# One kernel, a two-layer block and a hybrid layer: the chunk products of an HGRN2 recurrence cut into blocks of 32 keys

## The reference, cut to what matters

```python
def chunk_step(state, inp):
    qc, kc, vc, gc = inp
    b = jnp.cumsum(gc, axis=2)
    o_inter = jnp.einsum('bhck,bhkv->bhcv', qc * jnp.exp(b), state)
    diff = b[:, :, :, None, :] - b[:, :, None, :, :]
    decay = jnp.exp(jnp.where(causal, diff, -jnp.inf))
    scores = jnp.einsum('bhtk,bhsk,bhtsk->bhts', qc, kc, decay)
    o_intra = jnp.einsum('bhts,bhsv->bhtv', scores, vc)
    ...
```

## Time and profile before

| | |
|---|---|
| median of 3 runs | 2142.12 us (2141.5 to 2142.12) |
| the profiled execution | 2141.52 us, span from first to last instruction 2139.7 us |
| TensorE busy | 2123.4 us, 99% of the span |
| DVE, ACT, GpSimd (POOL) busy | 997.5, 744.0, 1133.7 us |
| mean granted TensorE clock | 0.999 |
| the recurrence | 77.7 to about 257 us |

### The profile page before, as it was taken

How to read it: one execution, slowest core, us unless ns; L and a number is a source line. 1 busy time by engine, 2 the same in 40 slices (tenths; PEclk the granted TensorE clock), 3 DMA queues, 4 the chain that set the end, 5 groups by cost and what they waited for, 6 DMA issues and landing times.

```text
span 2139.7 us, 26103 instructions
## 1 busy us (share of the span) xinstructions
PE 2123.4 (99%) x10184; PEld 1769.7 (83%) x10184; DVE 997.5 (47%) x1137; ACT 744.0 (35%) x850; POOL 1133.7 (53%) x814
## 2 busy tenths in 40 slices
PE   9999999999999999999999999999999999999998
PEld 7888888888888888978888888888888888888887
DVE  6255554555313165444545422744477545553226
ACT  5234442222223355544222232524543332222244
POOL 6565545555545433355555555544566555555553
PEclk9999999999999999999999999999999999999999
DMA  5221122222233212223222232222222222223321
GB/s 177 78 79 60 40 89 98 92 96 97 99 118 108 99 60 79 79 100 117 98 98 98 92 105 98 99 98 98 98 98 98 82 99 96 97 98 108 117 99 59
DMA packets 31567, 203.20 MB, mean 95 GB/s; under 512 B 3336, under 2 KB 5640, under 8 KB 7696
## 3 DMA queue, kind: packets, MB, share of 16 engines
q1 hardware_dynamic: 31504, 202.30, 27.3%
HBM read 200.19 MB, written 2.10 MB: 95 GB/s over the span
## 4 chain that ended last, share of the span: by engine, by line
PE 94%; DVE 2%; ACT 2%; POOL 1%; DMA 1%; issue 0%; SPq 0%; DVEq 0%; ACTq 0%; POOLq 0%
PE bank L1741 93%; POOL w_lo L604 1%; DMA raw<-wall 1%; ACT w_hi L680 0%; DVE x L1624 0%; PE bank L2078 0%; DVE sgate L1673 0%; DVE aqk L1452 0%; DVE bank L1449 0%; DVE rot L1450 0%; DVE ssq L1190 0%; DVE h L1674 0%; DVE ssq L1698 0%; PE bank L2099 0%; ACT rstd L680 0%
## 5 line engine op out<-in xcount | busy, mean ns | idle before, releaser
L585 POOL TENSOR_TENSOR w_lo<-raw,w_hi 128x512 fp32r<-128x512 f32 x680 | 979.9, 1472 | 875.9 <-ACT w_hi L680 875.9
L1741 PE MATMUL bank<-u_hi,w_hi 128*128 128x512 f32 (+1 forms) x1968 | 770.7, 392 | 2.2 <-DVE u_lo L1177 1.2
L1741 PE MATMUL bank<-u_lo,w_hi 128*128 128x512 f32 (+1 forms) x1968 | 761.9, 387 | 0.0
L680 ACT ACTIVATE w_hi<-raw 128x2048 fp32r<-128x2048 f32 (+1 forms) x189 | 358.5, 1897 | 957.5 <-PE bank L1741 949.4
L1741 PE MATMUL bank<-u_hi,w_lo 128*128 128x512 f32 (+1 forms) x1968 | 492.6, 388 | 0.1
L1741 PEld LDWEIGHTS bank<-u_hi,w_hi 128*128 128x128 f32 x1968 | 369.7, 188 | 81.2 <-issue 6.0
L1741 PEld LDWEIGHTS bank<-u_lo,w_hi 128*128 128x128 f32 x1968 | 369.7, 188 | 76.9 <-issue 2.9
L1741 PEld LDWEIGHTS bank<-u_hi,w_lo 128*128 128x128 f32 x1968 | 368.4, 188 | 76.2 <-POOL w_lo L604 0.2
L1741 PE MATMUL bank<-act_hi,w_hi 128*128 128x512 f32 x528 | 205.4, 389 | 0.0
L1741 PE MATMUL bank<-act_lo,w_hi 128*128 128x512 f32 x528 | 205.4, 389 | 0.0
L1221 DVE TENSOR_TENSOR sq<-bank,rstd 128x512 f32<-128x512 f32 x66 | 45.7, 692 | 269.0 <-PE bank L1741 236.8
(11 more groups left out here) (261 smaller groups left out, 2081.5 us busy)
## 6 DMA issues: line engine op xcount, KB each, us to landing
raw<-wall SPq DMA_DIRECT2D x186, 1024.0 KB, 4.8
out_t<-h SPq DMA_DIRECT2D x8, 256.0 KB, 2.5
h<-x_t SPq DMA_DIRECT2D x3, 512.0 KB, 8.1
raw<-wall SPq DMA_DIRECT2D x2, 256.0 KB, 4.6
h<-x_t SPq DMA_DIRECT2D x2, 256.0 KB, 3.9
raw<-wall SPq DMA_DIRECT2D x1, 512.0 KB, 7.2
lmask_f<-lmask_in SPq DMA_DIRECT2D x1, 512.0 KB
cs<-cs_in SPq DMA_DIRECT2D x1, 512.0 KB, 3.4
```

The lines of the kernel that those rows point to most:

```text
L585: ins = nc.gpsimd.tensor_tensor(w_lo[:, s, c], raw[:, s, c], w_hi[:, s, c].bitcast(F32), ALU.subtract)
L680: return nc.scalar.activation(out, in_, func, **k)
L1741: return nc.tensor.matmul(out, lhsT, rhs, start=start, stop=stop, skip_group_check=True)
```

## The change

Steps 0 to 4 of every pair (the diagonal and the spans 1, 2, 4, 8) are cut. No two tokens that these steps relate lie in different blocks of 32 tokens. So a chunk becomes four products, one for each block of 32 keys, each with that block's queries alone: 32 queries on the diagonal, 16 later-half queries in a level. A product's output starts at partition 32b.

The parts of the bank that are no longer written may hold anything. Therefore `take_products` no longer multiplies by the identity but copies through the diagonal's mask, and the two tiles of scores are set to zero once, behind the cast of the masks. The 17 warm-up products at the start go to the four quarters of bank 5 instead of to one of bank 7.

```diff
+CUT = 32
...
-                tt(s3, bank, ident[:].rearrange("p (n c) -> p n c", n=1).to_broadcast([P, TT, P]), ALU.mult)\
-                    .then_inc(lev_free, 1)
+                own = lmask[:, len(LEVELS):len(LEVELS) + 1, :].to_broadcast([P, TT, P])
+                nc.vector.copy_predicated(s3, own, bank).then_inc(lev_free, 1)
...
             cp(lmask[:], lmask_f[:]).then_inc(masks_ready, 1)
+            dve.wait_ge(masks_ready, 1)
+            for e in range(2):
+                ins = nc.vector.memset(scores_of_pair[e][:], 0.0)
+            ch.step(ins)
             cp(sel_r[:], sel[:]).then_inc(sel_ready, 1)
 
-            dve.wait_ge(masks_ready, 1)
+            ch.settle()
...
-            for _ in range(17):
-                ins = mm(PB[7][:, 0:P], ones[:], ones[:])
+            for n in range(17):
+                ins = mm(near(PB[5], n % TT), ones[:], ones[:])
...
                     if l == 0:
-                        ins = mm(near(PB[5 + a], c - TT * a), near(key[p % 2], c), near(q, c))
+                        for b in range(P // CUT):
+                            at = slice(CUT * b, CUT * (b + 1))
+                            ins = mm(near(PB[5 + a], c - TT * a)[at, at], near(key[p % 2], c)[:, at], near(q, c)[:, at])
...
                     else:
-                        ins = mm(level_bank(l)[:, c * P // 2:(c + 1) * P // 2], near(key[p % 2], c),
-                                 halves_of(near(q, c), l)[1])
+                        for b in range(P // CUT):
+                            at, to = slice(CUT * b, CUT * (b + 1)), c * P // 2 + b * CUT // 2
+                            ins = mm(level_bank(l)[at, to:to + CUT // 2], near(key[p % 2], c)[:, at],
+                                     halves_of(near(q, c)[:, at], l)[1])
```

## The result

| | before | after |
|---|---|---|
| median | 2141.84 us (4 runs, 2141.50 to 2142.12) | 2128.37 us (4 runs, 2127.92 to 2128.74) |
| the profiled execution | 2141.52 us, span 2139.7 | 2128.68 us, span 2126.9 |
| ratio after / before | | 0.9937, 95% interval 0.9925 to 0.9949 |

The changed kernel is faster by 13.5 us, 0.6%. The forecast was 2128.8 us, with a range of 2124 to 2137.

The account below looks back on a forecast made before the run. TensorE, busy 2123.4 of 2139.7 us, was taken to bound the kernel. Gains of 4.8 + 3.3 + 3.3 + 1.9 = 13.3 us in pairs 0 to 3 gave 2128.8 us against the median, range 2124 to 2137.

Parts of the forecast that it names:

- Part 1: Steps 0 to 4 of each pair on TensorE: 64 small load-and-matmul pairs take 0.62 us, gaining 0.96 us a step.
- Rival A: Steps 0 to 4: loads follow each other at 19.7 ns, gain 0.33 a step, 5.5 us in all, 2136.6; chance 0.17.
- rival C: Steps 0 to 4: strips do not overlap, 2.52 us a step, 2158, chance 0.03; fixed 25 ns pace, 2140, chance 0.02.
- Part 2, pairs 0 to 2: Recurrence: pair 0 gains 4.8 us, pairs 1 and 2 3.3 each, 1.5 lost in each to a new TensorE wait.
- Part 2, pair 3: Last pair of the recurrence: gains 1.9 us, between 1.6 and 2.0, held by GpSimd's fold and ACT's chain.
- rival D: Recurrence: after new waits TensorE's clock falls to 1.2 GHz for some 35 us, losing 17 us, 2146; chance 0.02.
- Part 3, DVE: DVE: predicated copies take 0.7 us against 0.69 for the multiply, added memsets hide in idle time; zero effect.
- The sum: Whole kernel: 4.8 + 3.3 + 3.3 + 1.9 = 13.3 us gained, 2128.8 against the median; chance 0.66.

Follow-up runs that it names:

- late_levels_whole: The changed kernel with levels 3 and 4 of pairs 1 to 3 as whole 128-key products again; 2129.43 us.
- sigmoid_late: The changed kernel with ACT's sigmoid of the next forget gates moved behind the head's root in pairs 1 and 2, DVE's use one step later; 2125.88 us.
- fill_wait: The changed kernel with eight unneeded 128x128 products of ones added behind level 4 of pair 3, where TensorE waits; 2128.05 us.
- folds_first: The changed kernel with GpSimd folding the keys of levels 1 to 3 in pair 3 ahead of the next panel's lower half; 2129.02 us.
- both_orders: The changed kernel with the reorderings of keys_behind_k and folds_first together; 2126.13 us.
- after_again: The changed kernel once more, unedited; 2128.49 us, ratio 0.9937 to the kernel before.
- keys_behind_k: The changed kernel with the transposes behind level 4 moved behind that step's projection k-steps in pairs 1 to 3; 2124.71 us.
- gate_late: keys_behind_k with the gates' silu of pair 3 on ACT, and its input on DVE, moved behind the head's root and level 3; 2125.04 us.

## Why the prediction was right

**Part 1, the price of a step.** Right, with the term a little too high. The forecast took level 5's 0.62 us for 64 pairs; they take 0.67, and on the diagonal 0.70, so a step gains 0.93 and not 0.96. Of the reading behind it, that a strip works by itself at 39 ns a pair, one part stood the test: neighbours in different strips overlap (0.67 against 1.43 us by order alone). The number failed: in one strip pairs follow each other at 22 ns and not at 39. Level 6, from which the 39 ns came, does not fit the 22: its products alternate between two strips, and its pairs follow at 19.7 ns, where strips that work by themselves at 22 ns would allow 11. So four strips in turn are twice as fast as one, two are hardly faster than one, and the simple picture of independent strips is not shown. A strip that is busy for 22 ns with a pair leaves room for 5.5 ns across four, and the first 28 loads of level 1 do stand within 0.21 us, under 8 ns apart:

```profile
82.19 0.32 PEld L1746 LDWEIGHTS bank<-q_dec,key 128*32 128x32 f32 x28 [0.35 <-issue]
```

The 0.67 us are 10 ns a pair on the average, so something other than the strip sets that pace; the runs don't say what. Rival A (two strips in turn, 1.26 us) and rival C (2.5 us, or 1.6 at a fixed pace) were wrong. The Trainium skill's page "TensorEngine Tiling (Array Packing)", section "Performance Considerations", puts some 60 cycles on every matmul, 25 ns by the forecast's estimate. As a spacing of neighbours the trace comes near it in one strip (22 ns) and contradicts it across strips (10 ns).

**Part 2, pairs 0 to 2.** Right: 4.57, 3.23 and 3.22 us against 4.8, 3.3 and 3.3. Pair 0's difference is the step: 5 x 0.93 = 4.65. The wait for DVE's scaling was put at 1.5 us and is 1.42 and 1.38. late_levels_whole and sigmoid_late show its cause from two sides.

**Part 2, pair 3.** This term failed: 1.20 us instead of 1.9, outside its own 1.6 to 2.0. Up to the transposes it even gave more than forecast. Counted from the pair's last large product ahead of the diagonal, level 2 starts 0.83 us earlier (forecast 0.66), and ACT's square 1.92 (forecast 1.62). By the same count the gain then is 1.92 at the transposes, 1.61 at level 5, only 0.63 at level 6, 1.21 at level 7. Between level 5 and level 6 the clock stands at 0.50. So what the forecast left out of this term is rival D, with its mechanism right and its size wrong: it was priced as 35 us at the lower level, and came as 3.4 us after the longest of the waits, with 1.3 us lost, of which 0.6 came back at the next place where another engine is late (TensorE waited 0.50 us for DVE there before, and not after). fill_wait, with the clock at 1.00, gains 31.86 - 29.94 = 1.92 in pair 3: the number of the forecast, but by another split. All of it is there at the transposes (forecast 1.62), and the up to 0.4 from a less crowded DVE did not come: TensorE still waits 0.49 us for it.

**Part 3, DVE.** Right. The timeline of the kernel after, the memsets and the first copies, against the earlier trace rows:

```profile
53.95 0.91 DVE L1405 MEMSET score_pair<- 128x1024 f32 x1 [0.28 <-DVE lmask L1402]
55.03 0.91 DVE L1405 MEMSET score_pair<- 128x1024 f32 x1 [0.16 <-issue]
...
77.82 1.37 DVE L1333 COPY_PREDICATED score_pair<-lmask,bank 128x512 f32<-128x512 uint8 x2 [21.61 <-PE bank L1746]
```

Two copies take 1.37 us, two multiplies took 1.51. The memsets cost 2 us in an idle stretch that still leaves 21.61.

**The sum.** 13.3 us were forecast. The two profiled executions differ by 12.8, 12.2 in the recurrence and 0.6 ahead of it; the medians differ by 13.5. So the agreement to 0.4 us is better than the terms deserve: the recurrence gave 1.1 less than forecast in the profiled run, and the rest is in the first loads, which vary by about a microsecond from run to run. Both profiles of after begin earlier than their partners of before, by 0.5 and 0.2 us. The diagonal of pair 0 begins at 77.05 to 78.04 us in the twelve profiles of kernels with the change, on the average at 77.4, and at 77.73 and 78.20 in the two without. The forecast put the new warm-up at zero; whether the change gains some tenths there is open.

## What to carry to other kernels

If a product covers blocks that don't interact, cut it into products of 32 stationary columns that go to the four strips of output rows in turn: the order of the loops, strip innermost, was here worth more than half of the gain. Before counting a gain on the bounding engine as so many steps times so much, follow at each step which other engine comes next; here 4.5 of 19 us (the 5.2 of the new waits less the 0.7 that was there before) ended in one wait for a chain on ACT. Then move what waits behind other work (17.2 us with it, 13.5 without), or take out of the chain what need not be in it.

## What the runs showed of the hardware that I had not expected

- The spacing of small fp32 products (pairs of load and matmul, 16 or 32 streamed columns): 10 ns when four strips of 32 take turns, 20 ns when two do, 22 ns mostly in one strip, 33 ns with two strips of 64, 107 to 111 ns with all 128 rows.
- A wait of 2.40 us in the middle of dense work was followed by 3.4 us of TensorE's lower clock, which began 1.4 us after the wait's end. After the waits of 1.42 and 1.38 us in pairs 1 and 2 it stayed at 1.00. The length of the wait alone does not tell: 2.74 us in folds_first were not followed by a fall, 1.16 and 0.82 us in both_orders were.
- The 16.0 us in 44 waits of the loads for "issue" are mostly no stalls. 20 new steps with the 0.35 us that stands ahead of every group of small loads make 7 us, and it is within the 1.31 us of a step.
- In pair 3 it is not one engine that is late. Freeing one of them brought nothing in the medians: folds_first lost 0.5 us against after_again and 1.4 beside keys_behind_k (both_orders), and gate_late lost 0.3 against keys_behind_k.
